# MLP and FFN up and gate panels with one 512-column matmul for both activation parts in a two-block fp32 network kernel on Trainium2

## The chip, the cores and the metric

One core of one Trainium2 chip runs the whole kernel. The metric is the device time of one execution in microseconds. A kernel's time is the median of its runs.

## The reference, cut to what matters

The input is 256 tokens of 1024 features, in float32. Two blocks follow each other. The first mixes tokens by attention and by a recurrence, then applies an MLP with 4096 hidden units. The second is a gated FFN with 2816 hidden units, a second mixer, and another gated FFN of the same size.

```python
hn = rms_norm(x, norm2_w[l])
x = x + jnp.square(jax.nn.relu(hn @ mlp_w1[l])) @ mlp_w2[l]

def swiglu(x, w_gate, w_up, w_down):
    return (jax.nn.silu(x @ w_gate) * (x @ w_up)) @ w_down
h = h + 0.5 * swiglu(rms_norm_2(h, ffn1_norm[l]), ffn1_w_gate[l], ffn1_w_up[l], ffn1_w_down[l])
```

## The kernel before

**Precision.** Every float32 product is made of three matmuls in the reduced format float32r. A weight W is split into `wh` (rounded) and `wl` (the remainder), an activation A into `acth` and `actl`. `three` (lines 573 to 576) adds wh x acth, wh x actl and wl x acth into the same place in PSUM. `feature_tile` (from line 583) does that for one tile of 128 output features: for each of 8 blocks of 128 input features, three matmuls whose stationary operand is a 128 x 128 piece of weight and whose moving operand is 256 columns, the tokens.

**Panels.** All weights stream through in panels of 1 MB, numbered in one order for the whole kernel. Three buffers each hold the raw panel (`raw`), its rounded part (`wh`) and its remainder (`wl`). SyncE issues the load of panel n once the remainder of panel n-3 is made (lines 385 to 394). ScalarE makes the rounded part (`hi`, line 1080, `hi_in_loop`, line 1086) once the panel has landed and TensorE is through with panel n-3. VectorE makes the remainder (`lo`, line 1400, `lo_in_loop`, line 1405). TensorE uses the panel once `lo_ready` has counted it.

**Up and gate panels.** `ffn_up` computes two tiles of 256 columns into one PSUM bank, which is 48 matmuls. MLP's up panels all use bank `ps[0]`. FFN's gate panels use `ps[0]`, its up panels `ps[1]`. Each engine's queue is in order and is written out by hand, step by step.

**Down panels.** `down` multiplies the hidden activations (stationary) by a panel of the second weight (moving, 512 columns) into the four banks of `acc4`: 8 places with 3 matmuls each, 24 matmuls. A `seed` (line 663) is one 512-column matmul with zero weights that opens a bank of `acc4`. TensorE takes the down panel of step s after the up panel of step s+1, so the hidden values have one panel of TensorE time to become ready.

**The hidden values, MLP.** ScalarE applies Relu to the bank into `ffa` (line 1272 for the first panel, 1281 in the loop) and sets `ff_act`, for which TensorE waits before it writes the bank again. VectorE squares (1706, 1717) into `ffs`, ScalarE rounds it into `midh` (`hidden_hi`, 1268), VectorE makes the remainder `midl` (`hidden_lo`, 1697) and sets `ff_lo`, for which the down panel waits. In the loop ScalarE's queue is Relu, `hi` of n+3, rounding, `hi` of n+4. VectorE's is `lo` of n+2, square, `lo` of n+3, remainder.

**The hidden values, FFN.** VectorE multiplies the gate bank by the norm's scale (`gate`, line 1734) and sets `ff_gate`. ScalarE applies Silu. VectorE multiplies it with the up bank (`product`, line 1729) and sets `ff_prod`. Rounding and remainder follow as in MLP. TensorE waits for `ff_gate` and `ff_prod` before it writes the gate and the up bank again.

**The first panel of each stage** starts while the norm still produces the activations, block by block. For its tile 0 `feature_tile` goes in another order (wh and wl by `acth`, then wh by `actl`, lines 586 to 591). In MLP the second up panel waits for the Relu of the whole first one. In the FFNs a `spread` of two small matmuls stands between the two tiles of the second panel.

Of the kernel before, what the change touches and what calls it, by code (L numbers as in the profile page):

```python
# [14 lines left out]
F32 = mybir.dt.float32  # L15
# [5 lines left out]
P = 128  # L21
# [73 lines left out]
def build(nc, a, out):  # L95
    ctx = ExitStack()
    with ctx:
# [10 lines left out]
        acth = sb("acth", [P, KT, T], F32R)  # L108
        actl = sb("actl", [P, KT, T], F32R)
# [95 lines left out]
        scale_bc = carve(15360, T)  # L205

        ps = [ctx.enter_context(nc.psum_tensor(f"ps{i}", [P, 512], F32)) for i in range(2)]
        acc4 = ctx.enter_context(nc.psum_tensor("acc4", [P, 4, 512], F32))
        ps += [acc4[:, i, :] for i in range(4)]
        ps += [ctx.enter_context(nc.psum_tensor(f"ps{i}", [P, 512], F32)) for i in (6, 7)]  # L210
# [111 lines left out]
        ff_gate = sem("ff_gate")  # L322
        ff_act = sem("ff_act")
# [227 lines left out]

        def up_bank(u, c):

            return ps[(6, 7, 0, 1)[2 * u + c]]
# [13 lines left out]
        def _(pe):  # L568
# [9 lines left out]
            def feature_tile(n, kt, c, out_, ah, al, norm=None):  # L578
# [14 lines left out]
                for k in range(kt):  # L593
                    last = three(out_, h[:, k, c * P:(c + 1) * P], l[:, k, c * P:(c + 1) * P],
                                 ah[:, k, :], al[:, k, :], k == 0, k == kt - 1)
                return last
# [282 lines left out]
            def ffn_up(n, b, norm=None, between=None):  # L879
                for c in range(2):  # L880
                    m = feature_tile(n, KT, c, ps[b][:, c * T:(c + 1) * T], acth, actl, norm)
                    if c == 0 and between is not None:
                        spread(between)
# [4 lines left out]
            ffn_up(ML, 0, 1)  # L888
            seed([3], 1)
            with pe.Fori(0, (ML_STEPS - 1) // 3) as i:  # L890
                for m in range(3):
# [3 lines left out]
                    pe.wait_ge(ff_act, i * 3 + (ML_F + m + 1))  # L895
                    ffn_up(n, 0)
# [8 lines left out]
            def spread(j):  # L905

                pe.wait_ge(diag_ready, j - 1)
                for tt in range(TT):
                    m = nc.tensor.matmul(ps[TURNED[0]][:, tt * P:(tt + 1) * P], cst[:, C_ONES:C_ONES + P], diag[:, tt, :],
# [3 lines left out]
            def swiglu(n0, f0, j):  # L913
                turn_rest(j)
                split(n0)
                ffn_up(n0, 0, j)
                seed([3], j)
                split(n0 + 1)
                ffn_up(n0 + 1, 1, None, j)
                with pe.Fori(0, (FF_STEPS - 1) // 2) as i:  # L920
                    for m in range(2):
                        n = n0 + 2 + 3 * m

                        for b, (read, r0) in enumerate(((ff_gate, f0 - F1_F), (ff_prod, f0))):
                            pe.wait_ge(lo_ready, i * 6 + (n + b + 1))
                            pe.wait_ge(read, i * 2 + (r0 + m + 1))
                            ffn_up(n + b, b)
# [138 lines left out]
        def _(act):  # L1066
# [199 lines left out]

            def hidden_hi(s):
# [3 lines left out]
            done(ML)  # L1271
            nc.scalar.activation(ffa, ps[0][:, :], ACT.Relu).then_inc(ff_act, 1)  # L1272
# [3 lines left out]
            with act.Fori(0, (ML_STEPS - 1) // 3) as i:  # L1276
                for m in range(3):
# [3 lines left out]
                    nc.scalar.activation(ffa, ps[0][:, :], ACT.Relu).then_inc(ff_act, 1)  # L1281
# [5 lines left out]
            def swiglu(n0, f0):  # L1287
# [3 lines left out]
                nc.scalar.activation(ffa, ffg, ACT.Silu).then_inc(ff_act, 1)  # L1291
                hi(n0 + 4)
# [3 lines left out]
                def two_steps(i, last):  # L1296
                    for m in range(2):
                        n = n0 + 2 + 3 * m
                        hi_in_loop(i, n + 3)

                        act.wait_ge(ff_gate, i * 2 + (f0 - F1_F + m + 2))
                        nc.scalar.activation(ffa, ffg, ACT.Silu).then_inc(ff_act, 1)
                        act.wait_ge(ff_prod, i * 2 + (f0 + m + 2))
                        hidden_hi((m + 1) % 2).then_inc(ff_hi, 1)
                        if not (last and m and n0 == F2):
                            hi_in_loop(i, n + 4)
# [82 lines left out]
        def _(dve):  # L1389
# [38 lines left out]
            def take_scales(j):  # L1428
                dve.wait_ge(bc_done, j - 1)
                link(nc.vector.tensor_copy(scale_bc, ps[TURNED[0]][:, 0:T]))  # L1430
# [272 lines left out]
            lo(ML + 1)  # L1703
            lo(ML + 2)
            dve.wait_ge(ff_act, ML_F + 1)
            nc.vector.tensor_tensor(ffs, ffa, ffa, ALU.mult).then_inc(ff_prod, 1)
            dve.wait_ge(ff_hi, ML_F + 1)
            hidden_lo(0).then_inc(ff_lo, 1)
            with dve.Fori(0, (ML_STEPS - 1) // 3) as i:
                for m in range(3):  # L1710
# [3 lines left out]
                    dve.wait_ge(ff_act, i * 3 + (ML_F + m + 2))  # L1714

                    dve.wait_ge(ff_lo, i * 3 + (ML_F + m + 1))
                    nc.vector.tensor_tensor(ffs, ffa, ffa, ALU.mult).then_inc(ff_prod, 1)
# [4 lines left out]
            def swiglu(n0, f0, meanwhile=None):  # L1722
                def product(at_panel, at_act, at_lo):

                    dve.wait_ge(panel_done, at_panel)
                    dve.wait_ge(ff_act, at_act)

                    dve.wait_ge(ff_lo, at_lo)
                    nc.vector.scalar_tensor_tensor(ffs, ps[1][:, :], 0.5, ffa, ALU.mult, ALU.mult).then_inc(ff_prod, 1)  # L1729

                def gate(at_panel):

                    dve.wait_ge(panel_done, at_panel)
# [208 lines left out]
```

## Time and profile before

| | us |
|---|---|
| median of 3 runs | 1014.34 |
| lowest and highest of them | 1013.87, 1015.89 |
| profiled execution, its own time | 1017.64 |
| span of its profile | 1015.8 |
| TensorE, VectorE, ScalarE busy | 997.7, 607.5, 491.1 |

The profile records one execution. Its rows give, for each instruction, the start, the duration, the engine, the source line, and the tiles written and read. PE is TensorE's matmuls, PEld its weight loads, DVE VectorE, ACT ScalarE. Matmuls are pipelined, so the duration of one is longer than the distance to the next one's start.

### The profile page before, as it was taken

How to read it: one execution, taken by the hardware profiler on the slowest of the kernel's cores; microseconds unless marked ns; L12 is line 12 of the kernel's file. 1: busy time of each engine (PE TensorE's matmuls, PEld its weight loads, DVE VectorE, ACT ScalarE, POOL GpSimd, SP SyncE). 2: the span in 40 equal slices, each digit the busy share in tenths (PEclk: the TensorE clock that was granted, in tenths of full speed). 3: DMA queues.
4: the chain of work that ended last, by engine and by line, in shares of the span. 5: the costliest groups of instructions: out<-in, count | busy, mean ns of one | idle time of the engine just before them, and what ended most of it. 6: DMA issues, size and time to landing. Idle time of an engine off the chain costs nothing.

```text
span 1015.8 us, 17060 instructions
## 1 busy us (share of the span) xinstructions
PE 997.7 (98%) x7106; PEld 932.9 (92%) x7106; DVE 607.5 (60%) x755; ACT 491.1 (48%) x611; POOL 57.6 (6%) x87
## 2 busy tenths in 40 slices
PE   6999999999999999999999999999999999999997
PEld 6989999998999999999999998998999899999996
DVE  4765676875645554586556656646655765545554
ACT  5675459634544434473434345444563463434342
POOL 4000000000200000021114001000000010000000
PEclk9999899999999999999999999999999999999999
DMA  9754243556555565537665654643324555555541
GB/s 285 230 168 125 84 130 120 195 179 207 186 181 192 174 198 189 183 125 237 205 209 177 212 186 140 208 125 125 118 91 150 183 176 190 185 183 187 183 157 41
DMA packets 128671, 173.13 MB, mean 170 GB/s; under 512 B 3120, under 2 KB 111936, under 8 KB 128624
## 3 DMA queue, kind: packets, MB, share of 16 engines
q1 hardware_dynamic: 127232, 168.56, 51.5%
q0 software_dynamic: 1392, 3.91, 1.3%
q8 instruction: 34, 0.56, 0.2%
q14 instruction: 13, 0.11, 0.0%
HBM read 171.40 MB, written 1.05 MB: 170 GB/s over the span
## 4 chain that ended last, share of the span: by engine, by line
PE 94%; DMA 2%; DVE 2%; ACT 1%; POOL 0%; issue 0%; SPq 0%; POOLq 0%; ACTq 0%; DVEq 0%
PE ps L574 20%; PE ps L576 20%; PE ps L575 20%; PE acc L574 8%; PE acc L575 8%; PE acc L576 8%; DMA raw<-in_w_in 2%; PE acc L955 2%; PE acc L977 1%; PE ps L707 1%; PE acc L963 1%; PE acc L678 1%; PE acc L834 1%; DVE wl L1400 1%; ACT acth L1117 1%; PE acc L690 1%
## 5 line engine op out<-in xcount | busy, mean ns | idle before, releaser
L574 PE MATMUL ps<-acth,wh 128*128 128x256 f32 x1592 | 456.4, 287 | 0.9 <-ACT xs L1272 0.5
L576 PE MATMUL ps<-acth,wl 128*128 128x256 f32 x1592 | 451.7, 284 | 0.0
L575 PE MATMUL ps<-actl,wh 128*128 128x256 f32 x1592 | 451.7, 284 | 0.0
L574 PEld LDWEIGHTS ps<-acth,wh 128*128 128x128 f32 x1592 | 306.7, 193 | 7.9 <-issue 5.4
L575 PEld LDWEIGHTS ps<-actl,wh 128*128 128x128 f32 x1592 | 306.7, 193 | 2.0 <-issue 0.5
L576 PEld LDWEIGHTS ps<-acth,wl 128*128 128x128 f32 x1592 | 306.6, 193 | 0.0
L1405 DVE TENSOR_TENSOR wl<-raw,wh 128x2048 fp32r<-128x2048 f32 x89 | 208.3, 2342 | 118.6 <-ACT wh L1086 118.6
L1086 ACT ACTIVATE wh<-raw 128x2048 fp32r<-128x2048 f32 x88 | 168.3, 1912 | 153.3 <-PE acc L576 79.4
L1080 ACT ACTIVATE wh<-raw 128x2048 fp32r<-128x2048 f32 x69 | 132.0, 1913 | 142.5 <-PE ps L576 116.1
L1400 DVE TENSOR_TENSOR wl<-raw,wh 128x2048 fp32r<-128x2048 f32 x68 | 155.5, 2288 | 39.6 <-ACT wh L1080 35.2
L574 PE MATMUL acc<-wh,midh 128*128 128x512 f32 x304 | 119.0, 391 | 0.1
L575 PE MATMUL acc<-wl,midh 128*128 128x512 f32 x304 | 118.7, 390 | 0.0
L576 PE MATMUL acc<-wh,midl 128*128 128x512 f32 x304 | 118.3, 389 | 0.0
L576 PEld LDWEIGHTS acc<-wh,midl 128*128 128x128 f32 x304 | 57.1, 188 | 12.2
L574 PEld LDWEIGHTS acc<-wh,midh 128*128 128x128 f32 x304 | 57.2, 188 | 11.3 <-issue 0.4
L575 PEld LDWEIGHTS acc<-wl,midh 128*128 128x128 f32 x304 | 57.2, 188 | 10.5
L1268 ACT ACTIVATE midh<-xs 128x512 fp32r<-128x512 f32 x38 | 23.8, 626 | 84.7 <-DVE xs L1729 84.7
L475 POOL TENSOR_SCALAR part<-ssq 128x1 f32<-128x1 f32 x12 | 2.9, 245 | 839.4 <-ACT arena L1105 350.6
L1697 DVE TENSOR_TENSOR midl<-xs,midh 128x512 fp32r<-128x512 f32 x38 | 27.7, 729 | 17.5 <-ACT midh L1268 17.5
L1281 ACT ACTIVATE xs<-ps 128x512 f32<-128x512 f32 x15 | 9.0, 598 | 57.5 <-PE ps L576 57.5
L1729 DVE SCALAR_TENSOR_TENSOR xs<-ps,xs 128x512 f32<-128x512 f32 x22 | 15.2, 691 | 32.9 <-PE ps L576 32.9
L1734 DVE TENSOR_TENSOR xs<-ps,arena 128x512 f32<-128x512 f32 x22 | 15.2, 690 | 26.0 <-PE ps L576 25.9
(265 smaller groups left out, 1012.1 us busy)
## 6 DMA issues: line engine op xcount, KB each, us to landing
raw<-in_w_in SPq DMA_DIRECT2D x37, 1024.0 KB, 5.4
raw<-in_mlp_w SPq DMA_DIRECT2D x32, 1024.0 KB, 5.3
raw<-in_ffn_w_gate SPq DMA_DIRECT2D x22, 1024.0 KB, 5.4
raw<-in_ffn_w_up SPq DMA_DIRECT2D x22, 1024.0 KB, 5.3
raw<-in_ffn_w_down SPq DMA_DIRECT2D x22, 1024.0 KB, 5.0
raw<-in_w_out SPq DMA_DIRECT2D x8, 1024.0 KB, 4.9
raw<-in_w_up_rnn SPq DMA_DIRECT2D x4, 1024.0 KB, 5.1
raw<-in_cmp_k_w SPq DMA_DIRECT2D x2, 1024.0 KB, 6.7
```

Source lines behind the costliest of these rows:

```text
L574: nc.tensor.matmul(out_, lh, rh, start=start, stop=False, **kw)
L575: nc.tensor.matmul(out_, lh, rl, start=False, stop=False, **kw)
L576: return nc.tensor.matmul(out_, ll, rh, start=False, stop=stop, **kw)
L955: m = nc.tensor.matmul(ps[2][:, tt * T:(tt + 1) * T], q[:, tt * P:(tt + 1) * P], kk, start=True, stop=True)
L1080: nc.scalar.activation(wh[:, n % R, :], raw[:, n % R, :], ACT.Copy).then_inc(hi_ready, 1)
L1086: nc.scalar.activation(wh[:, n % R, :], raw[:, n % R, :], ACT.Copy).then_inc(hi_ready, 1)
L1268: return nc.scalar.activation(midh[:, 2 * s:2 * s + 2, :].rearrange("p a t -> p (a t)"), ffs, ACT.Copy)
L1400: nc.vector.tensor_tensor(wl[:, n % R, :], raw[:, n % R, :], wh[:, n % R, :].bitcast(F32), ALU.subtract).then_inc(lo_ready, 1)
L1405: nc.vector.tensor_tensor(wl[:, n % R, :], raw[:, n % R, :], wh[:, n % R, :].bitcast(F32), ALU.subtract).then_inc(lo_ready, 1)
L1697: return nc.vector.tensor_tensor(midl[:, 2 * s:2 * s + 2, :].rearrange("p a t -> p (a t)"), ffs, midh[:, 2 * s:2 * s + 2, :].rearrange("p ...
L1729: nc.vector.scalar_tensor_tensor(ffs, ps[1][:, :], 0.5, ffa, ALU.mult, ALU.mult).then_inc(ff_prod, 1)
L1734: nc.vector.tensor_tensor(two(ffg), two(ps[0][:, :]), bc2, ALU.mult).then_inc(ff_gate, 1)
```

## The change

The two activation parts now lie in one tensor `actp`, so that one matmul can read both for one block of input features: its left 256 columns are wh x acth, its right 256 are wh x actl. The second matmul adds wl x acth to the left half. Each tile now takes a whole bank, so a panel takes two: `pair01` for MLP's up and FFN's gate panels, `pair67` for FFN's up panels. ScalarE copies the two right halves to SBUF, and VectorE adds the left halves to them. In MLP VectorE does Relu and square in one pass over the sum, and the Relu on ScalarE goes. In FFN ScalarE's `hi` of n+4 moves ahead of the rounding. The first panel of each stage keeps the three 256-column matmuls, in the left halves of its two banks. MLP's first panel is copied by VectorE tile by tile, and the second MLP panel waits per tile (`ff_half`, `ff_sum`). In the loop TensorE waits for `ff_sum` before each tile of an MLP up panel.

```diff
         wl = sb("wl", [P, R, PW], F32R)
-        acth = sb("acth", [P, KT, T], F32R)
-        actl = sb("actl", [P, KT, T], F32R)
+        actp = sb("actp", [P, 2, KT, T], F32R)
+        acth, actl = actp[:, 0], actp[:, 1]
         midh = sb("midh", [P, 6, T], F32R)
...
         scale_bc = carve(15360, T)
-        ps = [ctx.enter_context(nc.psum_tensor(f"ps{i}", [P, 512], F32)) for i in range(2)]
+        ffr = carve(8448, 2, T)
+        ffr2 = carve(8960, 2, T)
+        pair01 = ctx.enter_context(nc.psum_tensor("pair01", [P, 2, 512], F32))
         acc4 = ctx.enter_context(nc.psum_tensor("acc4", [P, 4, 512], F32))
-        ps += [acc4[:, i, :] for i in range(4)]
-        ps += [ctx.enter_context(nc.psum_tensor(f"ps{i}", [P, 512], F32)) for i in (6, 7)]
+        pair67 = ctx.enter_context(nc.psum_tensor("pair67", [P, 2, 512], F32))
+        ps = [pair01[:, i, :] for i in range(2)] + [acc4[:, i, :] for i in range(4)] + [pair67[:, i, :] for i in range(2)]
...
+        def spread_to(j):
+            return ps[TURNED[0]][:, 0:T] if j == 3 else pair01[:, 0, T:2 * T]
         def up_bank(u, c):
...
                                  ah[:, k, :], al[:, k, :], k == 0, k == kt - 1)
+                return last
+            def halved_tile(n, c, bank):
+                h, l = pv(n, KT, wh), pv(n, KT, wl)
+                cs = slice(c * P, (c + 1) * P)
+                for k in range(KT):
+                    nc.tensor.matmul(bank[:, :].rearrange("p (u t) -> p u t", u=2), h[:, k, cs], actp[:, :, k, :],
+                                     start=k == 0, stop=False)
+                    last = nc.tensor.matmul(bank[:, 0:T], l[:, k, cs], acth[:, k, :], start=False, stop=k == KT - 1)
                 return last
...
-            def ffn_up(n, b, norm=None, between=None):
+            def ffn_first(n, pair, norm):
                 for c in range(2):
-                    m = feature_tile(n, KT, c, ps[b][:, c * T:(c + 1) * T], acth, actl, norm)
+                    m = feature_tile(n, KT, c, pair[:, c, 0:T], acth, actl, norm)
+                    if c == 0 and n == ML:
+                        m.then_inc(ff_half, 1)
+                m.then_inc(panel_done, 1)
+            def ffn_up(n, pair, summed=None, between=None):
+                for c in range(2):
+                    if summed is not None:
+                        pe.wait_ge(ff_sum, summed + c)
+                    m = halved_tile(n, c, pair[:, c, :])
                     if c == 0 and between is not None:
...
             split(ML)
-            ffn_up(ML, 0, 1)
+            ffn_first(ML, pair01, 1)
             seed([3], 1)
...
-                    pe.wait_ge(ff_act, i * 3 + (ML_F + m + 1))
-                    ffn_up(n, 0)
+                    ffn_up(n, pair01, i * 6 + (2 * m + 1))
                     pe.wait_ge(lo_ready, i * 6 + (n + 2))
...
                 for tt in range(TT):
-                    m = nc.tensor.matmul(ps[TURNED[0]][:, tt * P:(tt + 1) * P], cst[:, C_ONES:C_ONES + P], diag[:, tt, :],
+                    m = nc.tensor.matmul(spread_to(j)[:, tt * P:(tt + 1) * P], cst[:, C_ONES:C_ONES + P], diag[:, tt, :],
                                          start=True, stop=True)
...
                 split(n0)
-                ffn_up(n0, 0, j)
+                ffn_first(n0, pair01, j)
                 seed([3], j)
                 split(n0 + 1)
-                ffn_up(n0 + 1, 1, None, j)
+                ffn_up(n0 + 1, pair67, None, j)
                 with pe.Fori(0, (FF_STEPS - 1) // 2) as i:
...
                             pe.wait_ge(read, i * 2 + (r0 + m + 1))
-                            ffn_up(n + b, b)
+                            ffn_up(n + b, (pair01, pair67)[b])
                         pe.wait_ge(lo_ready, i * 6 + (n + 3))
...
+            def right_half(to, pair):
+                return nc.scalar.activation(to, pair[:, :, T:2 * T], ACT.Copy)
             def hidden_hi(s):
...
             hi(ML + 2)
-            done(ML)
-            nc.scalar.activation(ffa, ps[0][:, :], ACT.Relu).then_inc(ff_act, 1)
             hi(ML + 3)
...
                     act.wait_ge(panel_done, i * 6 + (n + 1))
-                    nc.scalar.activation(ffa, ps[0][:, :], ACT.Relu).then_inc(ff_act, 1)
+                    right_half(ffr, pair01).then_inc(ff_right, 1)
                     hi_in_loop(i, n + 3)
...
                 nc.scalar.activation(ffa, ffg, ACT.Silu).then_inc(ff_act, 1)
+                done(n0 + 1)
+                right_half(ffr2, pair67).then_inc(ff_right, 1)
                 hi(n0 + 4)
...
                         n = n0 + 2 + 3 * m
+                        act.wait_ge(panel_done, i * 6 + (n + 1))
+                        right_half(ffr, pair01).then_inc(ff_right, 1)
                         hi_in_loop(i, n + 3)
...
                         nc.scalar.activation(ffa, ffg, ACT.Silu).then_inc(ff_act, 1)
+                        act.wait_ge(panel_done, i * 6 + (n + 2))
+                        right_half(ffr2, pair67).then_inc(ff_right, 1)
+                        if not (last and m and n0 == F2):
+                            hi_in_loop(i, n + 4)
                         act.wait_ge(ff_prod, i * 2 + (f0 + m + 2))
...
                         if not (last and m and n0 == F2):
-                            hi_in_loop(i, n + 4)
                             hi_in_loop(i, n + 5)
...
                 dve.wait_ge(bc_done, j - 1)
-                link(nc.vector.tensor_copy(scale_bc, ps[TURNED[0]][:, 0:T]))
+                link(nc.vector.tensor_copy(scale_bc, spread_to(j)))
...
             lo(ML + 1)
+            def squared(r):
+                flat_ = r.rearrange("p a t -> p (a t)")
+                return nc.vector.scalar_tensor_tensor(ffs, flat_, 0.0, flat_, ALU.max, ALU.mult)
+            def add_right(r, pair):
+                return nc.vector.tensor_tensor(r, pair[:, :, 0:T], r, ALU.add)
+            dve.wait_ge(ff_half, 1)
+            nc.vector.tensor_copy(ffr[:, 0, :], pair01[:, 0, 0:T]).then_inc(ff_sum, 1)
+            done(ML)
+            nc.vector.tensor_copy(ffr[:, 1, :], pair01[:, 1, 0:T]).then_inc(ff_sum, 1)
             lo(ML + 2)
-            dve.wait_ge(ff_act, ML_F + 1)
-            nc.vector.tensor_tensor(ffs, ffa, ffa, ALU.mult).then_inc(ff_prod, 1)
+            dve.wait_ge(ff_sum, 2)
+            squared(ffr).then_inc(ff_prod, 1)
             dve.wait_ge(ff_hi, ML_F + 1)
...
-                    dve.wait_ge(ff_act, i * 3 + (ML_F + m + 2))
+                    dve.wait_ge(ff_right, i * 3 + (m + 1))
+                    add_right(ffr, pair01).then_inc(ff_sum, 2)
+                    dve.wait_ge(ff_sum, i * 6 + (2 * m + 4))
                     dve.wait_ge(ff_lo, i * 3 + (ML_F + m + 1))
-                    nc.vector.tensor_tensor(ffs, ffa, ffa, ALU.mult).then_inc(ff_prod, 1)
+                    squared(ffr).then_inc(ff_prod, 1)
                     lo_in_loop(i, n + 3)
...
             def swiglu(n0, f0, meanwhile=None):
-                def product(at_panel, at_act, at_lo):
-                    dve.wait_ge(panel_done, at_panel)
+                def product(at_right, at_sum, at_act, at_lo):
+                    dve.wait_ge(ff_right, at_right)
+                    add_right(ffr2, pair67).then_inc(ff_sum, 1)
                     dve.wait_ge(ff_act, at_act)
+                    dve.wait_ge(ff_sum, at_sum)
                     dve.wait_ge(ff_lo, at_lo)
-                    nc.vector.scalar_tensor_tensor(ffs, ps[1][:, :], 0.5, ffa, ALU.mult, ALU.mult).then_inc(ff_prod, 1)
-                def gate(at_panel):
-                    dve.wait_ge(panel_done, at_panel)
-                    nc.vector.tensor_tensor(two(ffg), two(ps[0][:, :]), bc2, ALU.mult).then_inc(ff_gate, 1)
+                    nc.vector.scalar_tensor_tensor(ffs, ffr2.rearrange("p a t -> p (a t)"), 0.5, ffa, ALU.mult,
+                                                   ALU.mult).then_inc(ff_prod, 1)
+                def gate(at_right, at_sum):
+                    dve.wait_ge(ff_right, at_right)
+                    add_right(ffr, pair01).then_inc(ff_sum, 1)
+                    dve.wait_ge(ff_sum, at_sum)
+                    nc.vector.tensor_tensor(two(ffg), ffr, bc2, ALU.mult).then_inc(ff_gate, 1)
                 j = 2 if n0 == F1 else 4
+                r0 = ML_STEPS - 1 if n0 == F1 else ML_STEPS - 1 + 2 * FF_STEPS - 1
+                s0 = 2 * ML_STEPS if n0 == F1 else 2 * ML_STEPS + 2 * FF_STEPS - 1
                 lo(n0 + 1)
...
                 take_scales(j)
-                gate(n0 + 1)
+                done(n0)
+                nc.vector.tensor_tensor(two(ffg), pair01[:, :, 0:T], bc2, ALU.mult).then_inc(ff_gate, 1)
                 if meanwhile:
...
                 lo(n0 + 3)
-                product(n0 + 2, f0 + 1, f0)
+                product(r0 + 1, s0 + 1, f0 - F1_F + 1, f0)
                 dve.wait_ge(ff_hi, f0 + 1)
...
                         lo_in_loop(i, n + 2)
-                        gate(i * 6 + (n + 1))
+                        gate(i * 4 + (r0 + 2 * m + 2), i * 4 + (s0 + 2 * m + 2))
                         lo_in_loop(i, n + 3)
-                        product(i * 6 + (n + 2), i * 2 + (f0 + m + 2), i * 2 + (f0 + m + 1))
+                        product(i * 4 + (r0 + 2 * m + 3), i * 4 + (s0 + 2 * m + 3),
+                                i * 2 + (f0 - F1_F + m + 2), i * 2 + (f0 + m + 1))
                         dve.wait_ge(ff_hi, i * 2 + (f0 + m + 2))
```

## Rows read from the trace of the kernel before

**Rows 1.** The page, shares of the span, and the granted clock in 40 slices

```profile
PE 997.7 (98%) x7106; PEld 932.9 (92%) x7106; DVE 607.5 (60%) x755; ACT 491.1 (48%) x611; POOL 57.6 (6%) x87
...
PEclk9999899999999999999999999999999999999999
```

**Rows 2.** The page, the chain that ended last, by engine and by line

```profile
PE 94%; DMA 2%; DVE 2%; ACT 1%; POOL 0%; issue 0%; SPq 0%; POOLq 0%; ACTq 0%; DVEq 0%
PE ps L574 20%; PE ps L576 20%; PE ps L575 20%; PE acc L574 8%; PE acc L575 8%; PE acc L576 8%; DMA raw<-in_w_in 2%; PE acc L955 2%; PE acc L977 1%; PE ps L707 1%; PE acc L963 1%; PE acc L678 1%; PE acc L834 1%; DVE wl L1400 1%; ACT acth L1117 1%; PE acc L690 1%
```

**Rows 3.** Who waited for whom, whole span: us in total, times, longest

```profile
ACT wh L1086 <- PE ps L576: 73.9, 20, 3.9
...
PE ps L574 <- ACT xs L1272: 0.5, 1, 0.5
```

**Rows 4.** Timeline of PE, second MLP up panel: start us, us, what

```profile
264.06 0.28 PE L575 MATMUL ps<-actl,wh 128*128 128x256 f32 x1
...
269.58 0.28 PE L576 MATMUL ps<-acth,wl 128*128 128x256 f32 x1
```

**Rows 5.** Timeline of PE, the first MLP down panel and the seams around it

```profile
269.70 0.40 PE L574 MATMUL acc<-wh,midh 128*128 128x512 f32 x1
...
270.17 0.39 PE L576 MATMUL acc<-wh,midl 128*128 128x512 f32 x1
...
270.86 0.39 PE L576 MATMUL acc<-wh,midl 128*128 128x512 f32 x1
...
275.17 0.28 PE L574 MATMUL ps<-acth,wh 128*128 128x256 f32 x1
275.28 0.28 PE L575 MATMUL ps<-actl,wh 128*128 128x256 f32 x1
```

**Rows 6.** Timeline of PE, both FFNs, a seed alone between 256-column matmuls

```profile
446.49 0.40 PE L663 MATMUL acc<-mrgh,zero 128*128 128x512 f32 x1
446.73 0.28 PE L574 MATMUL ps<-acth,wh 128*128 128x256 f32 x1
446.84 0.27 PE L575 MATMUL ps<-actl,wh 128*128 128x256 f32 x1
...
447.07 0.28 PE L574 MATMUL ps<-acth,wh 128*128 128x256 f32 x1
...
827.07 0.40 PE L663 MATMUL acc<-mrgh,zero 128*128 128x512 f32 x1
827.31 0.28 PE L574 MATMUL ps<-acth,wh 128*128 128x256 f32 x1
```

**Rows 7.** Timeline around the end of MLP's first up panel

```profile
259.65 4.48 DVE L1400 TENSOR_TENSOR wl<-raw,wh 128x2048 fp32r<-128x2048 f32 x2
...
262.99 0.40 PE L663 MATMUL acc<-mrgh,zero 128*128 128x512 f32 x1
263.19 0.60 ACT L1272 ACTIVATE xs<-ps 128x512 f32<-128x512 f32 x1 [2.00 <-PE ps L576]
...
263.84 0.39 PE L574 MATMUL ps<-acth,wh 128*128 128x256 f32 x1 [0.45 <-ACT xs L1272]
```

**Rows 8.** Timeline of the last MLP step, up to its last down panel

```profile
427.47 1.91 ACT L1086 ACTIVATE wh<-raw 128x2048 fp32r<-128x2048 f32 x1
...
429.28 0.62 ACT L1268 ACTIVATE midh<-xs 128x512 fp32r<-128x512 f32 x1
429.42 2.29 DVE L1405 TENSOR_TENSOR wl<-raw,wh 128x2048 fp32r<-128x2048 f32 x1 [1.11 <-ACT wh L1086]
...
431.63 0.69 DVE L1697 TENSOR_TENSOR midl<-xs,midh 128x512 fp32r<-128x512 f32 x1
...
432.46 0.47 PE L574 MATMUL acc<-wh,midh 128*128 128x512 f32 x1
```

**Rows 9.** The page, costliest groups: VectorE's gate pass out of PSUM, us busy, mean ns

```profile
L1734 DVE TENSOR_TENSOR xs<-ps,arena 128x512 f32<-128x512 f32 x22 | 15.2, 690 | 26.0 <-PE ps L576 25.9
```

**Rows 10.** Windows, FFN1's steps: us, then PE PEld DVE ACT POOL busy, clock

```profile
446.73:600.00 153.27, 153.27 (x1107) 145.60 (x1106) 91.86 (x61) 63.38 (x47) 21.61 (x21) 1.00 0.65 205
```

More of the change, by code:

```diff
@@ L322, in build @@
         ff_gate = sem("ff_gate")
+        ff_right = sem("ff_right")
+        ff_sum = sem("ff_sum")
+        ff_half = sem("ff_half")
         ff_act = sem("ff_act")
```

## The prediction

> **What bounds the kernel now.** I read the shares first, then the chain of waits, then what TensorE waited for, and last the order of time around the panels that change. TensorE is busy for 98% of the span and its granted clock is in the 9s (full speed, 2.4 GHz) in all but the start; VectorE and ScalarE are at 60% and 48% [rows 1]. The chain that ended last runs 94% over PE, 59% of it over the three matmuls of lines 574 to 576 into `ps` [rows 2]. In the changed stages TensorE's wait for another engine is 0.5 us once, for a Relu, while ScalarE's splitting waits for TensorE, 73.9 us in 20 waits behind up panels alone [rows 3]. So in the stages touched the time is the number of matmuls times the gap from one start to the next. The durations of matmuls (0.28, 0.40 us) overlap and cost nothing by themselves; only starts count.
>
> **Gaps.** 256 columns: from 264.06 to 269.58 lie 46 gaps, 5.52 us, 120 ns each [rows 4]. 512 columns, settled: from 270.86 to 275.17 lie 19 gaps, 4.31 us, 227 ns each [rows 5]. 256 columns more cost 107 ns, which is 256 columns at 2.4 GHz, and 13 ns are paid per matmul whatever its length. That 13 ns is what joining two matmuls can save. At the seams the gaps differ: after a row of 256s the first two 512s take 0.47 us together, 235 each; the first five 1.16 us, 232 each; after the last 512 the first 256 takes 0.11 [rows 5]. The one kind of 512 that stands alone between 256s in this kernel, the seed at 446.49 (the other FFN's, at 827.07, has the same 0.24), has 0.24, then 0.11, then 0.23 for two: 0.58 us for one 512 and three 256s, the three at 113 each [rows 6].
>
> **Part 1, the halved panels.** MLP has 16 up panels, all but the first change: 15. Each FFN has 11 gate and 11 up panels, all but the first gate change: 21, twice. That is 57 panels of 2 x 8 steps, 912 steps. A step is three 256s now, 3 x 120 = 360 ns. Afterwards it is one 512 and one 256. The columns streamed are the same (768), one weight load and one matmul go. The trace shows no stream that alternates, so its gap is bounded: at the best 227 + 113 = 340 (the settled 512, and the faster 256s of rows 6); the plain sum of the settled gaps is 227 + 120 = 347; 0.24 + 0.11 = 350 is what the lone seed and its follower show; 235 + 120 = 355 if every 512 pays the seam of rows 5. The seed is the nearest row, since there too a 512 stands between 256s, but its next followers are short as well (0.58 us where settled gaps give 0.587). I take 349, between the seed's 350 and the settled 347: 11 ns x 912 = **10.0 us**. By the bounds: 18.2 us (340), 4.6 us (355).
>
> **Part 2, MLP's first panel.** Now the Relu of the whole bank starts at 263.19 and TensorE stands: seed at 262.99, next matmul at 263.84, 0.85 us where rows 6 have 0.24; its first gap is 0.22 (to 264.06 [rows 4]) where 0.12 is usual [rows 7]. 0.61 + 0.10 = **0.7 us**. Afterwards VectorE copies tile 0 while TensorE is on tile 1. VectorE is in two splits of 2.24 us from 259.65; the copy comes between them, at 261.9, and takes at most the 0.69 of a 512-column pass, so it ends by 262.6, ahead of 263.23 when the next panel can start. The copy of tile 1 has 2.8 us more, half a panel. Behind it is queued the second split, which then runs from some 263.9 to 266.1, then square 0.69, ScalarE's rounding 0.62, remainder 0.69 [rows 8], with three hand-overs 268.3. The down panel wants it at 263.23 + 5.58 = 268.8. That holds by 0.5 us; if it doesn't, the gain of this part goes back.
>
> **Part 3, more work on ScalarE and VectorE, 0 us.** Each halved FFN panel adds a ScalarE copy of 256 x 2 columns out of PSUM (0.60, as the Relu out of PSUM [rows 7]) and a VectorE add out of PSUM (0.69 [rows 9]); in MLP the copy takes the Relu's place and only the add is new. An FFN step (gate, up, down) lasts 2 x 5.76 + 24 x 0.228 = 17.0 us; VectorE is busy 91.86 of 153.27 us there, 10.2 us per step [rows 10], and would be at 11.6; ScalarE goes from 7.0 to 8.2. An MLP step lasts 11.2, and VectorE goes from 2 x 2.29 + 2 x 0.69 = 6.0 to 6.7 [rows 8]. What hides it: a gate or up bank is written again only after one or two other panels, at the least a down panel of 5.45 us. The new chain is 0.60 + 0.69 (+ 0.69 for the gate), about 2.2 us with hand-overs, and starts when VectorE has its split behind it. ScalarE's split of panel n+4 now stands ahead of the hidden rounding in FFN. That moves the hidden remainder about 1.7 us later and has some 10 us of room, since the down panel that reads it comes after another down and a gate and an up. The tightest place is MLP's last down panel: it waits for the remainder that ends at 432.32 and starts at 432.46 [rows 8]. The chain to it runs over ScalarE's split (from 427.47) and VectorE's split (from 429.42); the new add and the square are done by 429.1 in the shadow of the first of these, so it stays as it is. DMA issues are unchanged in number and size and follow the same splits. The seeds, the spread into another bank and the second wait in each MLP panel: 0, as the semaphore waits at panel ends now leave the gap at 0.12 [rows 4, 5]. If the cover were gone, each 0.1 us of wait per halved panel costs 5.7 us.
>
> **Sum.** -10.0 - 0.7 = -10.7 us, from the profiled execution's 1017.64 us (span 1015.8) to 1006.9. That execution is 3.3 us above the median of the runs, 1014.34; the saving is in TensorE's stream and carries over, so the median forecast is **1003.6 us**.
>
> **Rivals.**
> - *The fixed price is mostly not one per matmul* (0.14). The 13 ns comes from comparing up with down panels, which also differ in bank order and operands. For it: the first 512s at 235. Against: the settled 227 over 19 gaps, and the seed's short followers. A step is then 355: -4.6 - 0.7 = -5.3 us, 1009.0. The Trainium skill, "TensorE: Matmul & The Clock Gate", Back-to-back issue gap, speaks for a small gain: it gives N/2.4 + 2.5 ns as the gap, a fixed part of 2.5 ns. By that the change would bring 912 x 2.5 = 2.3 us, 3.0 with part 2; rows 4 with their 120 ns, not 109, don't agree with it in this kernel.
> - *The long matmul gives slack* (0.12). Each 256 after a 512 is as short as at the seam, the step is 340: -18.2 - 0.7, 995.4. Rows 6 speak for it, with 0.58 us; against it, the 512 in front took 0.24 there.
> - *The cover fails* (0.06). VectorE or ScalarE get late in every panel, and TensorE waits about 0.19 us in 57 panels, which eats it: 1014. Against: their shares and rows 3.
> - *Slower: the moving operand in two pieces* (0.06). The 512 reads two blocks of 256 columns, 2048 elements apart. No row shows such a read; all 512s of rows 5 and 6 read one block. If the change of piece cost another 13 ns like a change of matmul, on top of the 235 of the seam, a step is 235 + 13 + 120 = 368: +8 x 912 = +7.3, less 0.7, 1020.9. It decides from 360 ns per step on (with 120 behind it, from 240 for the 512). Against it: columns stream at exactly the clock's pace in both lengths, which leaves no sign of a reader that is short of time.
>
> **Numbers.** The forecast's case (a step of 345 to 353 ns, 999.9 to 1007.3) has 0.62. The range is 996.0 to 1010.5: the forecast's band, the 355 case and its spread, and half of the 340 case, about 0.82. About 0.2% (2 us) is what can be told from no change here, as the three runs lie 2 us apart. Faster by more: 0.62 + 0.14 + 0.12 = 0.88; within: 0.06; slower: 0.06.
>
> **What the profile after would show.** The timeline of a halved panel: a 512 start and a 256 start alternating, 16 steps in 5.58 us instead of 5.76; starts 0.227 to 0.24 and 0.11 to 0.12 apart. PE matmuls 7106 - 912 = 6194. No idle of TensorE before the second MLP panel, and MLP's last down still starts right behind the remainder it waits for. DVE about 57 x 0.69 = 39 us busier, ACT about 42 x 0.60 = 25. Wrong if the step measures 355 or more, if TensorE's waits list the new add, or if the granted clock changes.

## The result and the profile after

The changed kernel takes 1009.88 us (median of 5 runs, 1008.07 to 1010.84), the kernel before 1015.54 us (5 runs, among them the three told ahead). The ratio is 0.9943 with a 95% interval of 0.9931 to 0.9955: 5.7 us faster, where 10.7 us were forecast. The sign was right, and the gain lies in TensorE's gaps as forecast; the size was wrong.

The page of the changed kernel, engine times, clock and chain, against [rows 1, 2]:

```profile
PE 990.1 (98%) x6194; PEld 882.5 (88%) x6194; DVE 646.5 (64%) x814; ACT 511.4 (51%) x652; POOL 56.6 (6%) x87
...
PEclk9999999999999999999999999999999999999999
...
PE 95%; DVE 2%; issue 1%; ACT 1%; POOL 1%; DMA 0%; POOLq 0%; DVEq 0%; ACTq 0%
```

The matmuls are 6194, as counted. TensorE still sets the time. VectorE is 39.0 us busier, ScalarE 20.3 (not 25: where an instruction follows straight on another, the two overlap by 0.1 us and are counted once).

The span fell by 7.6 us, but 2.3 of these lie before the change: the first seed of MLP starts at 255.6 in the kernel before and at 253.3 here, and code up to there is the same. Over all kernels below it starts between 251.5 and 255.6. The traces show where this comes from. At about 101.4 us the granted clock of TensorE falls to its lower level (1.2 GHz) for 3.4 us in both kernels, and at 115.2 us once more for 3.4 us in the kernel before alone. In E3, E5 and E7 it does not fall there at all, and they have the earliest first seeds, 251.5 to 251.9. TensorE was busy for 60.6 of the 61.4 us ahead of 101.4 in each of these five, so its work does not tell them apart. Hence the stages are compared by themselves, from the starts of the seed matmuls (first of MLP, of FFN1, of FFN2) to the last matmul of all, worked out from the two traces:

| us | MLP | FFN1 and the mixer | FFN2 | sum |
|---|---|---|---|---|
| before | 183.41 | 380.66 | 188.86 | 752.94 |
| changed | 180.91 | 379.82 | 186.84 | 747.57 |

That is 5.4 us, and FFN1 gave 0.84 where FFN2, with the same panels, gave 2.03. Three things stand out.

**The step is longer than taken.** Timeline of PE in the changed kernel: the start of MLP's first halved panel, its first down panel (from 266.49), and the next up panel (from 271.97), the counterpart of [rows 4, 5] (start us, duration us, what):

```profile
260.94 0.39 PE L612 MATMUL pair<-actp,wh 128*128 128x512 f32 x1
261.17 0.28 PE L614 MATMUL pair<-actp,wl 128*128 128x256 f32 x1
261.28 0.40 PE L612 MATMUL pair<-actp,wh 128*128 128x512 f32 x1
...
266.49 0.39 PE L583 MATMUL acc<-wh,midh 128*128 128x512 f32 x1
...
271.97 0.39 PE L612 MATMUL pair<-actp,wh 128*128 128x512 f32 x1
272.20 0.28 PE L614 MATMUL pair<-actp,wl 128*128 128x256 f32 x1
272.31 0.40 PE L612 MATMUL pair<-actp,wh 128*128 128x512 f32 x1
272.54 0.28 PE L614 MATMUL pair<-actp,wl 128*128 128x256 f32 x1
272.66 0.40 PE L612 MATMUL pair<-actp,wh 128*128 128x512 f32 x1
272.90 0.28 PE L614 MATMUL pair<-actp,wl 128*128 128x256 f32 x1
273.02 0.40 PE L612 MATMUL pair<-actp,wh 128*128 128x512 f32 x1
273.26 0.28 PE L614 MATMUL pair<-actp,wl 128*128 128x256 f32 x1
273.37 0.40 PE L612 MATMUL pair<-actp,wh 128*128 128x512 f32 x1
...
277.61 0.40 PE L583 MATMUL acc<-wh,midh 128*128 128x512 f32 x1
```

The second halved panel lasts from 271.97 to 277.61, 5.64 us or 352.5 ns a step. Its steps are not alike: starts of the long matmuls lie 0.34, 0.35, 0.36, 0.35 apart. From the unrounded starts the gaps repeat every three steps as 236 + 113, 232 + 118, 241 + 120 ns, 353 on average, in MLP and in the FFNs.

The first halved panel, with the same matmuls in the same order, is faster: from 260.94 to 266.49, 5.55 us or 347 ns a step. It starts right behind the seed, and from its third step on its gaps are 230 + 117 ns to the end, without the cycle of three. The first tile of each FFN's second panel, which also starts right behind a seed, does the same (8 steps each). So alternation has two paces here. 32 of the 912 steps run at 347 ns, the other 880, which start behind a down panel, behind another halved panel or behind the spread, at 353.

The first down panel lasts from 266.49 to 271.97, 5.48, where it was 5.47 (269.70 to 275.17 in [rows 5]). Over the 32 down panels that can be compared the mean is 5484 ns after and 5468 before. The difference is not the same for all: MLP's others take 5467 as before, 15 of the 18 in the FFNs take 5503. Summed over all down panels of the trace it is 0.6 us, all of it in the FFNs.

**The stop at MLP's first panel is gone.** The same kernel's timeline where [rows 7] showed it:

```profile
259.56 0.42 DVE L1747 COPY arena<-pair 128x256 f32<-128x256 f32 x1
...
260.70 0.40 PE L682 MATMUL acc<-mrgh,zero 128*128 128x512 f32 x1
260.90 0.43 DVE L1749 COPY arena<-pair 128x256 f32<-128x256 f32 x1 [0.92 <-PE pair L585]
260.94 0.39 PE L612 MATMUL pair<-actp,wh 128*128 128x512 f32 x1
```

The copy of the first tile starts 1.1 us before the seed and ends before it, and the next matmul follows the seed after 0.24, not 0.85.

**A new wait stands in FFN1.** TensorE's waits for other engines, the counterpart of the second row in [rows 3], and the timeline of TensorE at that place:

```profile
PE pair L612 <- DVE wl L1440: 1.1, 1, 1.1
```

```profile
555.56 0.49 PE L612 MATMUL pair<-actp,wh 128*128 128x512 f32 x1 [1.06 <-DVE wl L1440]
```

VectorE's split of this panel came late. VectorE and GpSimd just before, in the kernel before and then in the changed one:

```profile
549.68 0.69 DVE L1729 SCALAR_TENSOR_TENSOR xs<-ps,xs 128x512 f32<-128x512 f32 x1 [1.68 <-PE ps L576]
551.07 2.20 DVE L1697 TENSOR_TENSOR midl<-xs,midh 128x512 fp32r<-128x512 f32 x1 [0.70 <-ACT midh L1268]
553.20 8.96 DVE L1405 TENSOR_TENSOR wl<-raw,wh 128x2048 fp32r<-128x2048 f32 x2
...
548.07 9.73 POOL L528 TENSOR_TENSOR arena<-cst,arena 128x2048 f32<-128x2048 f32 x2 [3.36 <-DMA arena<-in_rpb_rev]
```

```profile
544.03 0.69 DVE L1744 TENSOR_TENSOR arena<-pair,arena 128x512 f32<-128x512 f32 x1 [1.55 <-ACT arena L1295]
544.75 3.39 DVE L1779 SCALAR_TENSOR_TENSOR xs<-arena,xs 128x512 f32<-128x512 f32 x1
548.84 4.39 DVE L1732 TENSOR_TENSOR midl<-xs,midh 128x512 fp32r<-128x512 f32 x1 [0.70 <-ACT midh L1298]
553.15 4.48 DVE L1440 TENSOR_TENSOR wl<-raw,wh 128x2048 fp32r<-128x2048 f32 x2
...
542.92 9.76 POOL L533 TENSOR_TENSOR arena<-cst,arena 128x2048 f32<-128x2048 f32 x2 [4.23 <-DMA arena<-in_rpb_rev]
```

While GpSimd subtracts its two mask halves (4.7 and 5.1 us), VectorE's instructions with both operands in SBUF take longer, in both kernels. The hidden remainder takes 2.20 and 4.39 us instead of 0.69, and before the change two splits take 8.96 instead of 4.6. Those with one operand in PSUM take 0.69: the product L1729 before, the new add L1744 after. The change moved the product's operand from PSUM to SBUF, so it became one of those that are held up (3.39 us), and what stands behind it in VectorE's queue came later.

That is not all of it. Counted from GpSimd's start, the first of the two splits ends at 11.9 us in the kernel before and at 12.5 in the changed one, 0.6 later. TensorE comes to the panel that needs it at 12.5 before and at 11.4 in the changed kernel, 1.1 sooner. A margin of 0.6 us has become a wait. The panel and the gate panel ahead of it take 12.51 us instead of 11.29, so 1.2 us are lost.

### The profile page after: what moved, and what is told of

It reads as the page before. It is cut to its first block, busy times and chain, and to the rows that moved or that the text cites. A ratio compares the mean times of both kernels' runs of the same rounds, so it can differ in the third digit from the quotient of the medians.

```text
span 1008.2 us, 15482 instructions
## 1 busy us (share of the span) xinstructions
PE 990.1 (98%) x6194; PEld 882.5 (88%) x6194; DVE 646.5 (64%) x814; ACT 511.4 (51%) x652; POOL 56.6 (6%) x87
## 4 chain that ended last, share of the span: by engine, by line
PE 95%; DVE 2%; issue 1%; ACT 1%; POOL 1%; DMA 0%; POOLq 0%; DVEq 0%; ACTq 0%
PE pair L612 21%; PE pair L614 11%; PE pair L583 10%; PE pair L584 9%; PE pair L585 9%; PE acc L583 8%; PE acc L585 8%; PE acc L584 8%; PE acc L982 2%; PE acc L1004 1%; PE pair L726 1%; PE acc L990 1%; PE acc L697 1%; PE acc L853 1%; PE acc L709 1%
## 5 line engine op out<-in xcount | busy, mean ns | idle before, releaser
L612 PE MATMUL pair<-actp,wh 128*128 128x512 f32 x912 | 323.5, 398 | 1.1 <-DVE wl L1440 1.1
L614 PE MATMUL pair<-actp,wl 128*128 128x256 f32 x912 | 255.9, 281 | 0.0
L1440 DVE TENSOR_TENSOR wl<-raw,wh 128x2048 fp32r<-128x2048 f32 x89 | 203.8, 2290 | 68.0 <-ACT wh L1113 68.0
L612 PEld LDWEIGHTS pair<-actp,wh 128*128 128x128 f32 x912 | 171.3, 188 | 43.2 <-issue 1.4
L583 PE MATMUL pair<-actp,wh 128*128 128x256 f32 x680 | 197.3, 290 | 0.1
L585 PE MATMUL pair<-actp,wl 128*128 128x256 f32 x680 | 193.0, 284 | 0.0
L584 PE MATMUL pair<-actp,wh 128*128 128x256 f32 x680 | 193.0, 284 | 0.0
L1435 DVE TENSOR_TENSOR wl<-raw,wh 128x2048 fp32r<-128x2048 f32 x68 | 155.6, 2288 | 39.1 <-ACT wh L1107 35.5
L614 PEld LDWEIGHTS pair<-actp,wl 128*128 128x128 f32 x912 | 172.2, 189 | 1.4
L583 PEld LDWEIGHTS pair<-actp,wh 128*128 128x128 f32 x680 | 130.9, 193 | 5.4 <-issue 4.9
L584 PEld LDWEIGHTS pair<-actp,wh 128*128 128x128 f32 x680 | 131.0, 193 | 0.7 <-issue 0.5
L585 PEld LDWEIGHTS pair<-actp,wl 128*128 128x128 f32 x680 | 131.0, 193 | 0.0
L1295 ACT ACTIVATE arena<-pair 128x512 f32<-128x512 f32 x57 | 34.1, 598 | 177.9 <-PE pair L614 177.9
L1744 DVE TENSOR_TENSOR arena<-pair,arena 128x512 f32<-128x512 f32 x57 | 39.4, 691 | 93.4 <-ACT arena L1295 93.3
L583 PEld LDWEIGHTS acc<-wh,midh 128*128 128x128 f32 x304 | 57.1, 188 | 12.8 <-issue 0.4
L584 PEld LDWEIGHTS acc<-wl,midh 128*128 128x128 f32 x304 | 57.1, 188 | 10.7
```

The lines of the kernel that those rows point to most:

```text
L583: nc.tensor.matmul(out_, lh, rh, start=start, stop=False, **kw)
L584: nc.tensor.matmul(out_, lh, rl, start=False, stop=False, **kw)
L585: return nc.tensor.matmul(out_, ll, rh, start=False, stop=stop, **kw)
L612: nc.tensor.matmul(bank[:, :].rearrange("p (u t) -> p u t", u=2), h[:, k, cs], actp[:, :, k, :], start=k == 0, stop=False)
L614: last = nc.tensor.matmul(bank[:, 0:T], l[:, k, cs], acth[:, k, :], start=False, stop=k == KT - 1)
L1295: return nc.scalar.activation(to, pair[:, :, T:2 * T], ACT.Copy)
```

## The experiments

All but E7 start from the changed kernel. Stage sums are measured as in the table above.

### E1: the moving operand in one piece

```diff
-        actp = sb("actp", [P, 2, KT, T], F32R)
-        acth, actl = actp[:, 0], actp[:, 1]
+        actp = sb("actp", [P, KT, 2, T], F32R)
+        acth, actl = actp[:, :, 0, :], actp[:, :, 1, :]
...
-                    nc.tensor.matmul(bank[:, :].rearrange("p (u t) -> p u t", u=2), h[:, k, cs], actp[:, :, k, :],
+                    nc.tensor.matmul(bank[:, :], h[:, k, cs], actp[:, k, :, :].rearrange("p u t -> p (u t)"),
...
```

The lines left out let ScalarE and VectorE write the same values in the new layout.

> The changed kernel with the two activation parts interleaved by block of input features, so that the 512-column matmul reads one contiguous block of 512 columns and not two of 256. In the changed kernel a step (one 512, one 256) takes 353 ns and a panel 5.64 us. Theory 'two pieces': the split read costs the difference to 347; a step becomes 347 ns, a panel 5.55 us, the kernel 5.5 us faster than the changed one. Theory 'alternation': the price comes from alternating 512 and 256 columns; panel 5.64 us, time of the changed kernel (1009.9).

Measured: 1010.09 us, ratio to the kernel before 0.9947 (0.9934 to 0.9961); MLP 180.91 and FFN2 186.84 us, as in the changed kernel. The mean gap after a 512 is 236.0 ns in both, after a 256 116.9 in both. The two pieces cost nothing that can be seen; this theory, the slower rival of the prediction, falls.

### E2: eight long ones, then eight short ones, per tile

```diff
                 for k in range(KT):
                     nc.tensor.matmul(bank[:, :].rearrange("p (u t) -> p u t", u=2), h[:, k, cs], actp[:, :, k, :],
                                      start=k == 0, stop=False)
+                for k in range(KT):
                     last = nc.tensor.matmul(bank[:, 0:T], l[:, k, cs], acth[:, k, :], start=False, stop=k == KT - 1)
```

> The changed kernel with each tile's eight 512-column matmuls first and then its eight 256-column ones, instead of alternating. Theory 'alternation': inside a run the gaps settle at 227 and 120; with the seams of the kernel before (26 ns on entering the 512s, 9 ns back on leaving them) a panel is 5.55 + 2 x 0.017 = 5.58 us, 3.4 us less over 57 panels. Theory 'two pieces': the 512s stay at 233 to 240 each also in a row, the panel is 5.64 us or more and nothing is gained.

Measured: 1006.68 us, ratio 0.9915 (0.99 to 0.993). Sum of the stages 743.01, 4.6 less than the changed kernel. Timeline of PE, one up panel of MLP and the start of its down panel:

```profile
273.53 1.98 PE L612 MATMUL pair<-actp,wh 128*128 128x512 f32 x8
275.34 1.11 PE L615 MATMUL pair<-actp,wl 128*128 128x256 f32 x8
276.29 2.00 PE L612 MATMUL pair<-actp,wh 128*128 128x512 f32 x8
278.13 1.11 PE L615 MATMUL pair<-actp,wl 128*128 128x256 f32 x8
279.09 0.40 PE L583 MATMUL acc<-wh,midh 128*128 128x512 f32 x1
```

Eight 512s take 1.81 us (226 each) behind a down panel and 1.84 behind 256s. The panel takes 5.56, and the down panel is back at 5468 ns on the mean. So in panels that start behind a down panel the price came from the alternation, with the same matmuls and the same operands. It is not a fixed price of alternating, since the changed kernel's panel behind the seed alternates at 347 ns a step. The wait in FFN1 stays (its two panels lose 1.3 us).

### E3: GpSimd's mask in pieces

```diff
-                nc.gpsimd.tensor_tensor(nab[:, tt, :, :].rearrange("p h (i c) -> p (h i) c", c=64),
-                                        mask, bias, ALU.subtract).then_inc(nab_ready, 1)
+                whole = nab[:, tt, :, :].rearrange("p h (i c) -> p (h i) c", c=64)
+                for q in range(0, 4 * NH, 8):
+                    nc.gpsimd.tensor_tensor(whole[:, q:q + 8, :], mask[:, q:q + 8, :], bias[:, q:q + 8, :],
+                                            ALU.subtract).then_inc(nab_ready, 1)
...
-                    dve.wait_ge(nab_ready, 2)
+                    dve.wait_ge(nab_ready, 8)
...
-                            dve.wait_ge(nab_ready, 2)
+                            dve.wait_ge(nab_ready, 8)
```

> The changed kernel with GpSimd's two mask subtractions of 4.9 us each cut into eight of a quarter each. Theory 'GpSimd holds up VectorE': VectorE's product (3.39 us at 544.75, else 0.69) reads both operands from SBUF now and stood behind the long GpSimd instruction; in pieces none is held up by more than some 1.3 us at a time, and TensorE's wait of 1.1 to 1.2 us at 554.3 goes, 1.2 us less. Rival 'VectorE's queue has too little room with the new adds': the wait stays within 0.3 us of what it was.

Measured: 1009.22 us, ratio 0.9939 (0.9926 to 0.9953). That alone does not stand clear of the changed kernel, but the stage does: FFN1 with the mixer 378.58 against 379.82, 1.2 less, MLP and FFN2 within 0.04. VectorE and GpSimd at the same place:

```profile
542.95 0.88 DVE L1781 SCALAR_TENSOR_TENSOR xs<-arena,xs 128x512 f32<-128x512 f32 x1
544.54 1.00 DVE L1734 TENSOR_TENSOR midl<-xs,midh 128x512 fp32r<-128x512 f32 x1 [0.71 <-ACT midh L1300]
545.47 3.39 DVE L1442 TENSOR_TENSOR wl<-raw,wh 128x2048 fp32r<-128x2048 f32 x1
...
540.72 15.58 POOL L535 TENSOR_TENSOR arena<-cst,arena 128x512 f32<-128x512 f32 x8 [3.84 <-DMA arena<-in_rpb_rev]
```

The product takes 0.88 and no instruction is held up by more than 1.1 us. TensorE's wait for the split is no longer in the list. GpSimd pays for it: its work is spread over 15.6 us instead of 9.8.

### E4: MLP's first panel copied as a whole

```diff
-            dve.wait_ge(ff_half, 1)
+            done(ML)
             nc.vector.tensor_copy(ffr[:, 0, :], pair01[:, 0, 0:T]).then_inc(ff_sum, 1)
-            done(ML)
             nc.vector.tensor_copy(ffr[:, 1, :], pair01[:, 1, 0:T]).then_inc(ff_sum, 1)
```

> The changed kernel, but VectorE copies the tiles of MLP's first panel only when the whole panel is done. Theory of the prediction: TensorE stands again before the second MLP panel, for the copy of the first tile (about 0.4 us) and two hand-overs, 0.4 to 0.7 us more. Rival: reading by tile was hidden anyway, 0.

Measured: 1010.62 us, ratio 0.9954 (0.994 to 0.9968); MLP's stage 181.57 against 180.91, 0.66 more. TensorE at the place:

```profile
260.85 0.40 PE L682 MATMUL acc<-mrgh,zero 128*128 128x512 f32 x1
...
261.53 0.51 PE L612 MATMUL pair<-actp,wh 128*128 128x512 f32 x1 [0.28 <-DVE arena L1747]
261.72 2.28 DVE L1435 TENSOR_TENSOR wl<-raw,wh 128x2048 fp32r<-128x2048 f32 x1
261.87 0.28 PE L614 MATMUL pair<-actp,wl 128*128 128x256 f32 x1
```

The gap behind the seed is 0.68 instead of 0.24, and the first one after it 0.34 instead of 0.23, together 0.55 us. After this stop the same panel runs through the cycle of three steps (353 ns) and no longer at 347, which costs it another 0.10. So the pace depends on how the panel is entered, not on its data or its bank. Reading by tile is worth what the prediction gave it.

### E5: long ones of both tiles first, and the mask in pieces

`halved_long` holds a tile's 512-column matmuls, `halved_short` its 256-column ones. The mask's edit is that of E3.

```diff
                 for c in range(2):
...
-                    m = halved_tile(n, c, pair[:, c, :])
+                    halved_long(n, c, pair[:, c, :], range(KT))
                     if c == 0 and between is not None:
                         spread(between)
+                for c in range(2):
+                    m = halved_short(n, c, pair[:, c, :], range(KT))
```

> Both remedies: in a halved panel the sixteen 512-column matmuls of both tiles come first and then the sixteen 256-column ones, and GpSimd's mask subtraction is in eight pieces. If each entry into a run of 512s costs 26 ns and each exit gives 9 back, a panel has one such pair less than with grouping by tile (5.56 us): 5.543 us. Against the kernel before: 57 x (5.76 - 5.543) = 12.4 us, 0.7 from the first panel, and no wait of TensorE in FFN1: 13.1 us less, about 1002.5. Rival 'what is saved in the matmuls comes back as waits': the panels take 5.54 us, but TensorE's waits for VectorE in the FFN stages grow and less than 10 us is gained.

Measured: 1003.41 us, ratio 0.9878 (0.9862 to 0.9895), 12.8 us below the kernel before and 12.3 by the stages (MLP 179.52, FFN1 and mixer 376.46, FFN2 184.65). One panel:

```profile
270.62 3.79 PE L624 MATMUL pair<-actp,wh 128*128 128x512 f32 x16
274.24 2.08 PE L632 MATMUL pair<-actp,wl 128*128 128x256 f32 x16
276.16 0.40 PE L585 MATMUL acc<-wh,midh 128*128 128x512 f32 x1
```

Sixteen 512s in 3.62 (226 each), sixteen 256s in 1.92 (120 each), 5.54 together (347 a pair), and the down panel behind it takes 5467 ns, as in the kernel before. No wait of TensorE for VectorE appears in FFN1 or FFN2. This version beats both kernels.

### E6: two long, two short

```diff
-                for k in range(KT):
-                    nc.tensor.matmul(bank[:, :].rearrange("p (u t) -> p u t", u=2), h[:, k, cs], actp[:, :, k, :],
-                                     start=k == 0, stop=False)
-                    last = nc.tensor.matmul(bank[:, 0:T], l[:, k, cs], acth[:, k, :], start=False, stop=k == KT - 1)
+                for k in range(0, KT, 2):
+                    for j in (k, k + 1):
+                        nc.tensor.matmul(bank[:, :].rearrange("p (u t) -> p u t", u=2), h[:, j, cs], actp[:, :, j, :],
+                                         start=j == 0, stop=False)
+                    for j in (k, k + 1):
+                        last = nc.tensor.matmul(bank[:, 0:T], l[:, j, cs], acth[:, j, :], start=False, stop=j == KT - 1)
```

> The changed kernel with two 512s and two 256s in turn. It asks whether a change of length has a fixed price. Theory 'price per change': alternation has 16 changes each way in a panel and loses 16 x 6.9 = 110 ns to the settled sum of 5.547; with 8 the panel is 5.547 + 8 x 6.9 ns = 5.60 us. Rival 'price of a run's first matmuls, as at the down panels' (26 - 9 = 17 ns a pair of changes): 5.547 + 8 x 0.017 = 5.68 us.

Measured in one execution: 1005.46 us; MLP 179.66 and FFN2 184.79. One panel and its neighbour in PE's timeline:

```profile
272.31 0.62 PE L613 MATMUL pair<-actp,wh 128*128 128x512 f32 x2
272.76 0.40 PE L616 MATMUL pair<-actp,wl 128*128 128x256 f32 x2
273.00 0.63 PE L613 MATMUL pair<-actp,wh 128*128 128x512 f32 x2
...
277.87 0.40 PE L583 MATMUL acc<-wh,midh 128*128 128x512 f32 x1
```

The panel is 5.56 us, shorter than either theory had (5.60, 5.68), and the down panel behind it 5451 ns, 17 below the kernel before. So neither a fixed price per change nor the price of the down panel's entry describes it. Pairs cost hardly more than long runs; single alternation behind a down panel costs some 5 ns a step more (353 against 348). Why that is so, and why a panel behind a seed escapes it, is open.

### E7: the kernel before, with the mask in pieces

The edit is that of E3.

> The kernel before the change with GpSimd's mask subtraction in eight pieces. There TensorE did not wait behind it. Theory: the long GpSimd instructions cost the kernel before nothing, 0 (within 0.1%). Rival: they cost both kernels the same, 1 us less.

Measured: 1015.45 us, ratio 0.9995 (0.9985 to 1.0005); stages 183.40, 380.64, 188.86, sum 752.90 against 752.94. The long GpSimd instructions cost the kernel before nothing, so the 1.2 us of E3 are there only with the change.

### E8: the product reads its sum from PSUM

```diff
-                    add_right(ffr2, pair67).then_inc(ff_sum, 1)
+                    left = pair67[:, :, 0:T]
+                    nc.vector.tensor_tensor(left, left, ffr2, ALU.add).then_inc(ff_sum, 1)
...
-                    nc.vector.scalar_tensor_tensor(ffs, ffr2.rearrange("p a t -> p (a t)"), 0.5, ffa, ALU.mult,
+                    nc.vector.scalar_tensor_tensor(ffs.rearrange("p (a t) -> p a t", t=T), left, 0.5,
+                                                   ffa.rearrange("p (a t) -> p a t", t=T), ALU.mult,
                                                    ALU.mult).then_inc(ff_prod, 1)
```

> The changed kernel, but VectorE's add in the FFN up panels writes its sum back into PSUM, and the product reads it from there, so that only one of its operands lies in SBUF. GpSimd's long instructions stay. Theory 'two operands in SBUF stand behind GpSimd': the product under GpSimd's first mask instruction takes 0.69 us and not 3.39, while the hidden remainder and the split (two SBUF operands) are still held up. Rival 'any VectorE instruction is slowed while GpSimd works': the product stays above 2 us.

Measured in one execution: 1009.96 us. VectorE and GpSimd:

```profile
545.01 0.69 DVE L1780 SCALAR_TENSOR_TENSOR xs<-pair,xs 128x512 f32<-128x512 f32 x1
546.60 2.06 DVE L1732 TENSOR_TENSOR midl<-xs,midh 128x512 fp32r<-128x512 f32 x1 [0.89 <-ACT midh L1298]
548.58 8.97 DVE L1440 TENSOR_TENSOR wl<-raw,wh 128x2048 fp32r<-128x2048 f32 x2
...
543.43 9.76 POOL L533 TENSOR_TENSOR arena<-cst,arena 128x2048 f32<-128x2048 f32 x2 [4.49 <-DMA arena<-in_rpb_rev]
```

The product takes 0.69 under GpSimd's first instruction; the remainder and the split behind it are held up instead, 2.06 and some 6.8 us, as in the kernel before. So it is the instructions with two SBUF operands that are held up while GpSimd works. The split now ends 11.9 us after GpSimd's start, 0.6 sooner than in the changed kernel, but TensorE comes at 11.2 and still waits. That wait is listed with 0.7 us, and the two panels lose 1.0. The time alone does not show the remedy: E1, whose product is that of the changed kernel, lost 0.9 at this place. The Trainium skill, "SBUF — State Buffer", Who interferes with whom, says just this: a VectorE instruction with two SBUF inputs contends with a GpSimd one that reads SBUF, while one with at most one SBUF input, outside the two-port modes, does not. Both traces agree (0.69 against 2.06 to 4.39 us).

## Why the prediction was wrong

- **What bounds the kernel.** Right: TensorE's gaps set the time before and after, 98% busy in both.
- **Part 1, the step of 349 ns.** This is the step that failed. It was put between the seed's 350 and the settled 347 and used for all 912 steps; 880 of them measure 353. The seed's row stands for panels that start right behind a seed, and there the step is indeed 347 ns, but these are 32 steps. In all others 236 + 113, 232 + 118 and 241 + 120 follow each other, and the third costs 361. So 912 steps bring some 6.5 us and not 10.0. E1 shows that the split operand has no part in it, E2 that the order has. Why the cycle of three arises stays open. The rival with 355 was nearer than the forecast.
- **Part 1, what was left out.** The seam to the down panel was not given a term. After alternation it costs 36 ns more in most down panels of the FFNs and nothing in MLP, 0.6 us in all.
- **Part 2, 0.7 us.** Right: the gap behind the seed fell from 0.85 to 0.24, and the slow first gap behind it (0.22) is gone. E4, which brings a stop back, costs 0.66. The margin for the first down panel held, no wait appears there.
- **Part 3, 0 us.** Wrong in one place by 1.2 us. I counted VectorE's load and its chain and never asked where the product's operands lie, nor read GpSimd's rows. Undisturbed steps show no wait, as said. Under GpSimd's two instructions the margin was 0.6 us before; the split now ended 0.6 later, behind the held-up product, and TensorE came 1.1 sooner. E3 takes the wait away and gives the 1.2 us back; E7 shows that the kernel before loses nothing there. MLP's last down panel stays as it was, 0.44 us behind the matmul ahead of it in both kernels.
- **The slower rival** (a price of the two pieces) fell with E1. The rival that the cover fails in every panel fell too; it fails in one of 57.
- **The fixed part per matmul.** The settled gaps of 120 and 226 stand again in E5's panels, so the 13 ns are there. The fixed part of 2.5 ns that the Trainium skill gives for a matmul by itself ("TensorE: Matmul & The Clock Gate", Back-to-back issue gap), by which the change would have brought 3.0 us, does not fit them.

In sum: 6.5 - 0.6 + 0.7 - 1.2 = 5.4 us, which is what the stages show (752.94 - 747.57). The median of 1009.88 us is 6.3 above the forecast of 1003.6: 5.0 for the smaller gain, and 1.2 because the kernel before has a median of 1015.54 over five runs and not the 1014.34 that the forecast started from.

## What to carry to other kernels

Joining two matmuls saved the full 13 ns each here where matmuls of one length stood together, and only some 7 where they alternated behind a down panel: group long and short ones, since these kernels can choose the order inside an accumulation. When an edit moves an operand of a VectorE instruction from PSUM to SBUF, look up what GpSimd does at that time, and try its SBUF instructions in short pieces. Compare stages by marks in the trace and look at the granted clock, since what lies ahead of the change moved by up to 4 us here with up to two stretches of 3.4 us at the lower clock.

## What the runs showed that was not expected

Single alternation of 512 and 256 columns has two paces in one kernel: 347 ns a step where it starts right behind a seed, and else a cycle of three steps (349, 350 and 361 ns). Twos (5.56 us a panel) come close to runs of sixteen (5.54) and even shorten the next down panel by 17 ns. Cutting GpSimd's 9.8 us into eight pieces stretches it to 15.6 us but takes 1.2 us off the kernel.
